# A fused decoder trunk in split fp32r: the FFN's first product runs all w_hi matmuls of a group, then all w_lo

## The reference

```python
def conv_ffn(x, w_in, conv_w, conv_b, w_out):      # w_in: 1024 x 5632, w_out: 2816 x 1024
    up, gate = jnp.split(x @ w_in, 2, axis=-1)
    up = causal_depthwise_conv(up, conv_w) + conv_b  # three taps
    return (jax.nn.gelu(up) * gate) @ w_out
x = layer_norm(DEEPNORM_ALPHA * x + conv_ffn(x, ...), ln_g, ln_b)
```

## Time and profile before

| | us |
|---|---|
| median of three runs | 615.63 |
| the profiled execution | 615.26 |
| its span on the core | 613.5 |
| granted TensorE clock, share of full | 0.997 |
| TensorE busy | 598.8 |
| VectorE busy | 478.3 |
| ScalarE busy | 331.8 |
| GpSimd busy | 56.5 |

### The profile page before, as it was taken

How to read it: one execution, slowest core, us unless ns; L and a number is a source line. 1 busy time by engine, 2 the same in 40 slices (tenths; PEclk the granted TensorE clock), 3 DMA queues, 4 the chain that set the end, 5 groups by cost and what they waited for, 6 DMA issues and landing times.

```text
span 613.5 us, 8717 instructions
## 1 busy us (share of the span) xinstructions
PE 598.8 (98%) x3284; PEld 506.9 (83%) x3284; DVE 478.3 (78%) x865; ACT 331.8 (54%) x540; POOL 56.5 (9%) x79
## 2 busy tenths in 40 slices
PE   8999999999999999999999999999999999999995
PEld 6887777798888888889888788788988888888894
DVE  4899974876778887777679997868777777777756
ACT  5657875446444445455435587953655555444530
POOL 5200000300000000000520013022000000000002
PEclk9999999999999999999999999999999999999998
DMA  8768542254566665554535565223835555555501
GB/s 304 259 238 310 202 142 70 70 191 153 206 206 206 205 205 195 189 190 185 204 148 196 205 207 188 89 70 136 275 109 183 192 204 202 188 190 183 198 2 68
DMA packets 69238, 109.84 MB, mean 179 GB/s; under 512 B 2332, under 2 KB 47692, under 8 KB 68684
## 3 DMA queue, kind: packets, MB, share of 16 engines
q1 hardware_dynamic: 68332, 105.09, 50.0%
q0 software_dynamic: 576, 4.19, 1.7%
q10 hardware_dynamic: 288, 0.00, 0.0%
HBM read 108.23 MB, written 1.05 MB: 178 GB/s over the span
## 4 chain that ended last, share of the span: by engine, by line
PE 83%; DVE 13%; ACT 2%; issue 1%; DVEq 0%; ACTq 0%
PE wide L1163 13%; PE wide L1165 13%; PE wide L1164 13%; PE score L1365 11%; PE score L1368 6%; PE outb L1365 5%; PE turn L1365 5%; DVE w_lo L867 5%; PE turn L1368 3%; PE outb L1368 3%; DVE qT L986 2%; DVE kT L986 2%; PE turn L1267 1%; ACT w_hi L670 1%; PE score L1176 1%
## 5 line engine op out<-in xcount | busy, mean ns | idle before, releaser
L867 DVE TENSOR_TENSOR w_lo<-raw,w_hi 128x2048 fp32r<-128x2048 f32 (+1 forms) x118 | 213.0, 1827 | 61.6 <-ACT w_hi L670 61.4
L670 ACT ACTIVATE w_hi<-raw 128x2048 fp32r<-128x2048 f32 (+1 forms) x126 | 181.9, 1483 | 33.7 <-PE wide L1165 14.3
L1163 PE MATMUL wide<-w_hi,xT 128*128 128x512 f32 (+1 forms) x256 | 96.6, 377 | 0.5 <-DVE w_lo L933 0.5
L1163 PE MATMUL wide<-w_hi,oT_hi 128*128 128x512 f32 x240 | 95.3, 397 | 0.2 <-DVE oT_lo L1110 0.2
L1164 PE MATMUL wide<-w_lo,oT_hi 128*128 128x512 f32 x240 | 93.7, 391 | 0.0
L1165 PE MATMUL wide<-w_hi,oT_lo 128*128 128x512 f32 x240 | 93.5, 390 | 0.0
L1165 PE MATMUL wide<-w_hi,xT 128*128 128x512 f32 (+1 forms) x256 | 93.2, 364 | 0.0
L1164 PE MATMUL wide<-w_lo,xT 128*128 128x512 f32 (+1 forms) x256 | 93.0, 363 | 0.0
L1365 PE MATMUL score<-xT,w_hi 128*128 128x512 f32 x288 | 71.9, 391 | 0.0
L798 ACT ACTIVATE qT<-kT,conv_cols 128x256 f32<-128x256 f32 x36 | 21.7, 602 | 87.8 <-DVE kT L1076 87.8
L1365 PEld LDWEIGHTS score<-xT,w_hi 128*128 128x128 f32 x288 | 52.8, 188 | 10.1
(11 more groups left out here) (182 smaller groups left out, 870.0 us busy)
## 6 DMA issues: line engine op xcount, KB each, us to landing
raw<-in_ffn_w_in SPq DMA_DIRECT2D x44, 1024.0 KB, 5.1
raw<-in_ffn_w_out SPq DMA_DIRECT2D x22, 1024.0 KB, 4.9
raw<-in_a_w_qkv SPq DMA_DIRECT2D x9, 1024.0 KB, 5.5
raw<-in_w_kv_shared SPq DMA_DIRECT2D x8, 1024.0 KB, 5.2
raw<-in_a_w_o SPq DMA_DIRECT2D x4, 1024.0 KB, 5.0
raw<-in_b_w_q SPq DMA_DIRECT2D x4, 1024.0 KB, 6.0
raw<-in_b_w_o SPq DMA_DIRECT2D x4, 1024.0 KB, 4.9
raw<-in_a_w_qkv SPq DMA_DIRECT2D x4, 512.0 KB, 8.3
```

Source lines behind the costliest of these rows:

```text
L670: ins = nc.scalar.activation(w_hi[c % RING][:, part], raw[c % RAW_RING][:, part], ACT.Copy)
L867: ins = nc.vector.tensor_tensor(w_lo[c % RING][:, part], raw[c % RAW_RING][:, part], w_hi[c % RING][:, part].bitcast(F32), ALU.subtract)
L1163: nc.tensor.matmul(dst, a_hi, b_hi, start=start, stop=False, skip_group_check=True)
```

## The change

In groups 1 to 9 of both layers TensorE no longer finishes a feature tile before it begins the next. It opens all four banks: 32 w_hi matmuls of 512 columns, tile by tile (up 0, up 1, gate 0, gate 1), then 32 w_lo matmuls of 256 columns in the same order of tiles. The number and the forms of the matmuls stay. The semaphores stay and are raised in the same order, but each at the end of its tile's w_lo matmuls. The waits stand ahead of each tile's w_hi matmuls, and the wait for the gate chunk's w_lo ahead of the gate tiles' w_hi. In group 1 the token transposes move from behind up 0 to behind the w_hi matmuls of up 1. Group 10 keeps its order in a function of its own. The other engines' programs are not touched.

```diff
-                def features(banks, slot, free, done0, together, between=None):
+                def with_hi(bank, slot, tt):
+                    for kt in range(KT):
+                        nc.tensor.matmul(by_two(bank), w_hi[slot][:, tile_cols(kt, tt)], xT[:, :, kt, :], start=kt == 0,
+                                         stop=False, skip_group_check=True)
+
+                def with_lo(bank, slot, tt):
+                    for kt in range(KT):
+                        last = nc.tensor.matmul(by_two(bank)[:, 1, :], w_lo[slot][:, tile_cols(kt, tt)], xT_hi[:, kt, :],
+                                                start=False, stop=kt == KT - 1, skip_group_check=True)
+                    return last
+
+                def features(up_slot, gate_slot, gate_chunk, free, between=None):
                     for tt in range(2):
                         if free is not None:
-                            pe.wait_ge(*free[tt])
...
+                            pe.wait_ge(up_summed, free + tt)
+                        with_hi(up_bank[tt], up_slot, tt)
+                    if between:
+                        between()
+                    pe.wait_ge(lo_done, gate_chunk + 1)
+                    for tt in range(2):
+                        if free is not None:
+                            pe.wait_ge(gate_summed, free + tt)
+                        with_hi(gate_bank[tt], gate_slot, tt)
+                    with_lo(up_bank[0], up_slot, 0).then_inc(up0_done, 1)
+                    with_lo(up_bank[1], up_slot, 1).then_inc(chunk_used, 1)
+                    with_lo(gate_bank[0], gate_slot, 0).then_inc(gate0_done, 1)
+                    with_lo(gate_bank[1], gate_slot, 1).then_inc(chunk_used, 1)
```

More of the change, by code:

```diff
@@ L1354, in _, with tile_cols, by_two @@
                             last.then_inc(tokens_done, 1)
-                def features(banks, slot, free, done0, together, between=None):
+                def tile_cols(kt, tt):
+                    return slice(kt * 2 * P + tt * P, kt * 2 * P + (tt + 1) * P)
+                def by_two(bank):
+                    return bank[:, :].rearrange("p (a q) -> p a q", a=2)
+                def with_hi(bank, slot, tt):
+                    for kt in range(KT):
+                        nc.tensor.matmul(by_two(bank), w_hi[slot][:, tile_cols(kt, tt)], xT[:, :, kt, :], start=kt == 0,
+                                         stop=False, skip_group_check=True)
@@ new lines, in features, with last_features @@
+                    with_lo(gate_bank[0], gate_slot, 0).then_inc(gate0_done, 1)
+                    with_lo(gate_bank[1], gate_slot, 1).then_inc(chunk_used, 1)
+                def last_features(banks, slot, free, free0, done0):
+                    for tt in range(2):
+                        pe.wait_ge(free, free0 + tt)
+                        for kt in range(KT):
+                            last = product(by_two(banks[tt])[:, 0, :], w_hi[slot][:, tile_cols(kt, tt)],
+                                           w_lo[slot][:, tile_cols(kt, tt)], xT_hi[:, kt, :], xT_lo[:, kt, :],
+                                           kt == 0, kt == KT - 1)
@@ L1374, in features @@
                         last.then_inc(done0 if tt == 0 else chunk_used, 1)
-                        if tt == 0 and between:
-                            between()
                 def first_group_transposes():
@@ L1410, in ffn_group @@
                     second = peeled == "second"
[L1411 to L1418, removed]
+                    cu, cg = ffn_chunk(layer, i, 0), ffn_chunk(layer, i, 1)
+                    free = sums_before(t, layer) - 1
+                    pe.wait_ge(lo_done, cu + 1)
+                    if peeled == "last":
+                        last_features(up_bank, cu % RING, up_summed, free, up0_done)
+                        pe.wait_ge(lo_done, cg + 1)
+                        last_features(gate_bank, cg % RING, gate_summed, free, gate0_done)
+                    else:
+                        features(cu % RING, cg % RING, cg, None if second else free, first_group_transposes if second else None)
                     if second:
```

## The result

The changed kernel takes 619.28 us (median of 14 runs, 618.12 to 620.90), the kernel before 615.75 (14 runs beside them, 615.16 to 621.02). The ratio is 1.0044, 95% interval 1.0029 to 1.0059: slower by less than the half per cent that the chances were set by. The profiled run took 618.65, with a span of 616.8 against 613.5.

The account below looks back on a forecast made before the run. TensorE's matmul issue was taken to bound the kernel, with a VectorE and GpSimd chain last at layer 0's end. Loop gain -1.02 plus +3.52 gave +2.50 on 615.63, 618.1 us; own range 617.5 to 618.9, all cases 614.1 to 619.5.

Parts of the forecast that it names:

- GpSimd keeps the port: End of layer 0: GpSimd holds the SBUF port over all three parts, net +3.55 us, 619.2; chance 0.12.
- the likeliest case: Whole kernel: loop gain of 1.02 us against 3.52 lost at layer 0's end, 618.1; chance 0.50 for +1.9 to +3.3.
- The loop: FFN groups: fewer tails behind w_lo runs save 0.06 us per middle group, 1.02 us in sum.
- VectorE held to T + 8.46: Middle groups: VectorE's first sum starts 8.46 us after the group's start T, 2.66 us later than before; nobody in the loop waits.
- Steps 1 to 5: End of layer 0: late VectorE's two L1110 alternate with GpSimd's queued parts; TensorE restarts at 301.05 against 299.00, residual 3.52 us later.
- gain kept: End of layer 0: first GpSimd part misses L1110, or VectorE is served for all three operations; 614.2 to 615.0; chance 0.27.
- step 5: End of layer 0: TensorE restarts at 301.05; L876 behind part three delays residual L903 by 3.52 us, TensorE alone by 2.05.
- Step 6: From L903 to layer 1's transposes: a serial chain, so nothing swallows the 3.52 us.
- the idle time of more than 1 us ahead of the transposes: Sign at layer 1's start: TensorE idles more than 1 us ahead of the transposes.
- Layer 1's end: Behind layer 1's last group GpSimd has no split and VectorE's idle time takes in its delay: nothing lost.
- The loop stall: FFN loop, group 2: banks or w_lo come late, up to +0.5 us; chance 0.06, shared with more idle time than counted.
- The slack of 0.15 us in group 2: Group 2 of layer 0: TensorE would need gate 0's bank about 0.15 us after the semaphore arrives, so the wait is covered.

Follow-up runs that it names:

- The run without L876: The changed kernel, with VectorE writing zeros into the half chunk instead of computing its w_lo at the end of layer 0: 617.83 us, ratio 1.0024.
- The repeat: The changed kernel itself run once more, nothing altered, for a second profile: 619.59 us, ratio 1.0039 to the kernel before.
- the pairs: Against the changed kernel, 16 w_hi then 16 w_lo matmuls for the two up tiles, then the same for the gate tiles: 618.52 us, ratio 1.0022.
- the first four experiments: ScalarE's split moved ahead on the changed kernel (614.48 us) and kernel before (615.83); moved back on the kernel before (620.44); matmuls by pairs of tiles (618.52).
- the next four: Pairs of tiles with ScalarE's split ahead (614.39 us); kernel before, VectorE late (621.45); changed kernel, zeros for w_lo (617.83); new order in layer 1 only (615.84).
- the three kernels with the part moved ahead: ScalarE splits both halves of layer 1's first chunk ahead of the last group's gelus: changed kernel 614.48 us, kernel before 615.83, order by pairs of tiles 614.39.
- the two kernels of the old order that were made late by hand: Kernel before with ScalarE's second half split later, so GpSimd starts later: 620.44 us; kernel before with three extra VectorE fills in layer 0's group 8: 621.45 us.

## Why the prediction was right, and where it was not

The time forecast was 618.1, its own range 617.5 to 618.9; measured were 619.28 and 618.65 in the profiled run. The median lies inside the range over all cases (614.1 to 619.5), but 0.4 above the forecast's own, and by the number alone it would be *GpSimd keeps the port* (619.2). It is the traces that show that the likeliest case came, by its own steps, with a second cost on top in some executions.

- **The loop.** 16.55 per middle group and 3.83 for 32 w_lo were forecast, and both are in the trace. The first product behind a w_lo run costs 0.03 more, once a group. Of 1.02 us, 0.89 shows: 0.44 and 0.33 in the account, and 0.06 of group 9 in its third and in its last row. What is missing is a stall of 0.13 in group 2 of layer 1. The isolated gap of the Trainium skill, "TensorE: Matmul & The Clock Gate", section "Back-to-back issue gap", by which the order would be worth nothing, does not fit to this digit: the 0.06 a group is in the rows.
- **VectorE held to T + 8.46.** Measured 8.41, from group 5 on, in both layers.
- **Steps 1 to 5.** GpSimd starts at 295.83 (forecast 295.67), the first L1110 ends at 298.52 (298.35), the second at 301.01 (300.90), TensorE restarts at 301.16 (301.05), L903 starts at 304.25 (304.18). Group 10 began 0.16 later than before, which is what most of them are late by. The order of service, one for each side in the order of asking, was the step on which *GpSimd keeps the port* and *gain kept* hung. POOL's three parts without a pause, each L1110 ending with one of them, decide it. The run without L876 shows the second half of step 5, at a clock of 1.00.
- **Step 6.** From group 9 to the transposes 3.53 was lost, without group 9's own gain 3.59, where 3.52 was forecast. This nearness is partly luck: TensorE, slowed by its clock, came as late as VectorE, and the idle time of more than 1 us ahead of the transposes, one of the signs that were named, was not there. The repeat, with the clock at 1.00, is the better witness: idle time 1.35, loss up to the transposes 3.4.
- **Layer 1's end.** Nothing lost, as forecast.

Four things were sized wrong or not seen.

- **The second meeting.** The steps ended with L924 and took it at its old length. But in the repeat, counted from the first of the second products (295.23, 295.88 before), VectorE's first L924 was moved by 3.4 us (307.98 against 305.23) and GpSimd's fourth part, which follows TensorE through ScalarE's split, only by 2.0 (308.16 against 306.79). So that part, behind both L924 before, came between them. The second L924 takes 2.88 us instead of 0.75 there, and from the transposes to layer 1's group 1 the repeat needs 128.89 us instead of 127.26, 1.6 more. The median lies 1.2 above the forecast; that this is the reason fits the two kinds of runs (medians 618.5 and 619.7) but has one profile for each. The steps should have carried GpSimd's next part along too, since each operation that is moved meets a new neighbour.
- **The clock.** No step had it. In the first profile TensorE stood still for 2.2 us and then needed 0.43 us for each of seven products instead of 0.23, and somewhat more than that for those beside them, 1.6 us in all. They just fitted under VectorE's delay. Without L876, where they don't, the runs with the lower clock are 1.9 us longer.
- **The loop stall.** It was given 0.5 us at most and 6 in 100. It was there in three profiles of this order, with 0.13, 0.9 and 1.1 us, each time after a late raw load (ScalarE waited 2.57, 2.73 and 3.52 us). The slack of 0.15 us in group 2 was read rightly, but from one execution, in which the load had come earlier. The new order leaves VectorE no lead with which to take up a late load.
- **The edge.** The 0.8 us that *gain kept* would have needed is room on the late side: part one would have to start behind L1110's asking, at 296.47 instead of 295.67. How little it takes on the early side was not worked out: 0.60 us, from rows 7 and 10. A change that makes VectorE only somewhat later, as the pairs did, already pays for most of the meeting.

The kernel before may fall over this edge too. Of the 30 runs of it beside the first four experiments, and of the 30 beside the next four, 8 each took 618.62 us or more (up to 622.75) and the others 615.06 to 617.62, whereas the three kernels with the part moved ahead, in whatever order, stay within 2.7 us each. That these sixteen are runs in which a late load let the meeting happen is argued from this and not shown: there is no profile of one.

## What to carry to other kernels

Before an engine that is off the critical path is made later, list what the other engine on its SBUF port does at that time, one operation after the other and until the two are apart again, for a row of three long operations of GpSimd held three short ones of VectorE, one each. If the meeting can't be avoided by the order you want, move the other side: one line on ScalarE took 0.8% off the changed kernel, where the change itself is worth 0.2% by its sum. And read the slack of a wait from more than one execution when a load stands behind it.

## What the runs showed of the hardware

- **Service at the port goes by the order of asking**, across both engines: with GpSimd's next part already queued when VectorE asks, and VectorE's next operation queued when a part ends, they take turns. A held L1110 ends 0.28 us after the part, and a held L876 takes 3.4 us for 1.1 of work. The Trainium skill, "SBUF — State Buffer", section "Who interferes with whom", has the port held for a whole instruction by whoever issues first; these traces agree, and add who is next.
- **The clock after a stall differs between executions of the same kernel.** After an idle time of 2.2 us the granted clock was 0.56 over the stretch from 301.30 to 305.10 us in one profile and 1.00 over the same stretch in another. In the two kernels of the old order that were made late by hand it stayed at 1.00, after 1.7 and 3.2 us of idle time.
- **A run of 256-column products leaves 0.03 us behind it**, whether of 8, 32 or 96: the six 512-column products that follow take 1.39 us in each case, where six undisturbed ones take 1.36.
- **An operation with one of its two inputs in PSUM was not held.** L1105 of group 10 took its usual 0.42 us at 296.29 in the changed kernel, in the middle of GpSimd's first part (295.83 to 298.24), while L1110 right behind it, with both inputs in SBUF, was.
